# Retention scores: key's rounded part and remainder stacked on 128 partitions

## The reference, cut to what matters

```
def retention(q, k, v, pos):
    q = rope(q, pos)
    k = rope(k, pos) * (dk ** -0.5)
    ...
    def step(state, inp):
        qi, ki, vi = inp
        inner = jnp.einsum('bhid,bhjd->bhij', qi, ki) * decay_mat
        o = jnp.einsum('bhij,bhjv->bhiv', inner, vi) + jnp.einsum('bhid,bhdv->bhiv', qi, state) * q_decay
        ...
```

## Time and profile before

| | us |
|---|---|
| median of 3 runs | 2582.18 (2581.99 to 2584.53) |
| the profiled execution: its own time | 2581.51 |
| the profiled execution: its span | 2579.7 |
| PE busy | 2559.3 (99% of the span) |
| DVE busy | 1103.8 (43%) |
| POOL busy | 1051.2 (41%) |
| ACT busy | 1003.7 (39%) |
| 1976 to 2110 us: PE busy | 133.61 of 134.00, granted clock 1.00 |
| 1976 to 2110 us: ACT, DVE, POOL busy | 73.38, 62.52, 43.41 |

### The profile page before, as it was taken

One profiled execution on the slowest core, in us unless ns is written; L12 is line 12 of the kernel. 1 busy time (PEld: TensorE's weight loads), 2 busy tenths in 40 slices (PEclk: granted clock), 3 DMA queues, 4 the chain that ended last, 5 costly groups with the idle time before them and its releaser, 6 DMA issues.

```text
span 2579.7 us, 35875 instructions
## 1 busy us (share of the span) xinstructions
PE 2559.3 (99%) x12914; PEld 2106.1 (82%) x12914; DVE 1103.8 (43%) x2138; ACT 1003.7 (39%) x1619; POOL 1051.2 (41%) x464
## 2 busy tenths in 40 slices
PE   8999999999999999999999999999999999999998
PEld 7888888887777888888889888889777778888887
DVE  7444336754444135644315544223454455422212
ACT  5222337544454334322334322223555554322321
POOL 0444454342233444544455444453122335344443
PEclk9999999999999999999999999999999999999999
DMA  7455532222222323455532554333112223233232
GB/s 297 157 190 192 179 129 76 66 74 83 90 90 74 106 98 123 168 194 191 179 122 79 199 195 147 99 125 110 50 49 83 86 85 113 68 98 97 94 103 97
DMA packets 78284, 313.15 MB, mean 121 GB/s; under 512 B 9040, under 2 KB 11728, under 8 KB 68720
## 3 DMA queue, kind: packets, MB, share of 16 engines
q1 hardware_dynamic: 65376, 238.09, 27.5%
q10 hardware_dynamic: 12816, 73.80, 8.1%
HBM read 309.72 MB, written 2.13 MB: 121 GB/s over the span
## 4 chain that ended last, share of the span: by engine, by line
PE 96%; DVE 2%; ACT 1%; DMA 0%; POOL 0%; issue 0%; SPq 0%; DVEq 0%; ACTq 0%
PE bank L1955 26%; PE bank L1957 26%; PE bank L1956 26%; PE bank L2007 2%; PE bank L2008 2%; PE bank L2009 2%; PE pair L2223 1%; PE bank L2404 1%; PE pair L2295 1%; PE bank L2282 1%; PE pair L2432 1%; PE bank L2312 1%; PE bank L2412 1%; ACT h_hi L637 0%; PE bank L2488 0%; PE pair L2481 0%
## 5 line engine op out<-in xcount | busy, mean ns | idle before, releaser
L557 POOL TENSOR_TENSOR w_lo<-raw,w_hi 128x1024 fp32r<-128x1024 f32 x412 | 1013.1, 2461 | 1445.6 <-ACT w_hi L596 1445.6
L596 ACT ACTIVATE w_hi<-raw 128x1024 fp32r<-128x1024 f32 x420 | 443.9, 1059 | 1080.9 <-PE bank L1957 1034.2
L1955 PE MATMUL bank<-h_hi,w_hi 128*128 128x512 f32 x2064 | 820.2, 397 | 0.0
L1957 PE MATMUL bank<-h_hi,w_lo 128*128 128x512 f32 x2064 | 804.9, 390 | 0.0
L1956 PE MATMUL bank<-h_lo,w_hi 128*128 128x512 f32 x2064 | 803.8, 389 | 0.0
L1955 PEld LDWEIGHTS bank<-h_hi,w_hi 128*128 128x128 f32 x2064 | 388.0, 188 | 92.7 <-issue 16.3
L1957 PEld LDWEIGHTS bank<-h_hi,w_lo 128*128 128x128 f32 x2064 | 387.5, 188 | 82.7
L1956 PEld LDWEIGHTS bank<-h_lo,w_hi 128*128 128x128 f32 x2064 | 388.1, 188 | 77.2 <-issue 1.2
L1390 DVE TENSOR_TENSOR prod<-bank,rstd 128x512 f32<-128x512 f32 x87 | 60.1, 691 | 428.8 <-PE bank L1957 417.9
L1955 PE MATMUL bank<-act_hi,w_hi 128*128 128x512 f32 x616 | 239.6, 389 | 0.0
L1956 PE MATMUL bank<-act_lo,w_hi 128*128 128x512 f32 x616 | 239.6, 389 | 0.0
(11 more groups left out here) (444 smaller groups left out, 3026.1 us busy)
## 6 DMA issues: line engine op xcount, KB each, us to landing
raw<-slabs_dram SPq DMA_DIRECT2D x420, 512.0 KB, 3.7
adaw<-ada_dram ACTq DMA_DIRECT2D x62, 1024.0 KB, 6.7
ada<-ada_dram SPq DMA_DIRECT2D x8, 1024.0 KB, 20.5
x<-xt_dram SPq DMA_DIRECT2D x4, 512.0 KB, 5.6
adaw<-ada_dram SPq DMA_DIRECT2D x2, 1024.0 KB, 23.6
fneg<-fneg_scratch ACTq DMA_DIRECT2D x4, 512.0 KB, 3.8
sq<-fneg_scratch ACTq DMA_DIRECT2D x4, 512.0 KB, 3.6
w<-w_dram SPq DMA_DIRECT2D x1, 2048.0 KB, 7.9
```

Source lines behind the costliest of these rows:

```text
L557: nc.gpsimd.tensor_tensor(wl[s][:], raw[s][:], wh[s][:], ALU.subtract).then_inc(lo_done, 1)
L596: nc.scalar.activation(wh[s][:], raw[s][:], ACT.Copy).then_inc(hi_done, 1)
L1955: MM(out, wh[s][:, k], a, start=first and j == 0, stop=False)
L1957: ins = MM(out, wl[s][:, k], a, start=False, stop=end and j == len(tiles) - 1)
```

## The change

A buffer `rks[a]` now holds both halves of a head's key on all 128 partitions: the rounded part on the head's own 64 partitions, the remainder on the other 64. The rounded query is written twice (`rqh[a]`, once on each half), the query's remainder once (`rql[a]`), and the other half of `rql[a]` is set to zero once before the first pair. A score is then two matmuls over all 128 rows: `rks` by `rqh` gives hi by hi plus lo by hi, and `rks` by `rql` gives hi by lo. The sum has the same three terms as before. In a group the two matmuls of head 0 come first, then the two of head 1; before, the heads alternated.

`rq_lo_b` lies where `ssacc` is, a buffer that isn't in use during the retention. The first hunk only puts that place on a boundary of 512 bytes.

```
--- before.py
+++ after.py
@@ -224,6 +224,8 @@
             wh.append(sb(f"w_hi{s}", [P, KT, P], F32R))
         for s in range(RING):
             slab_buffers(s)
+        cursor[0] += -cursor[0] % 512
+        ssacc_at = cursor[0]
         ssacc = sb("ssacc", [P, T])
         sq = sb("sq", [P, 2, T])
         rstd = sb("rstd", [P, T])
@@ -312,6 +314,9 @@
 
 
         cursor[0] = shared
+        end, cursor[0] = cursor[0], ssacc_at
+        rql_b = sb("rq_lo_b", [P, T], F32R)
+        cursor[0] = end
         onh = sb("on_hi", [P, NP, T], F32R)
         onl = sb("on_lo", [P, NP, T], F32R)
         orh = sb("or_hi", [P, NP, T], F32R)
@@ -360,8 +365,9 @@
         cursor[0] = m2_at
         rqr = sb("rqr", [P, 2, T])
         rqk = sb("rqk", [P, 2, T])
-        rqkh = sb("rqk_hi", [P, 2, T], F32R)
-        rqkl = sb("rqk_lo", [P, 2, T], F32R)
+        rqh = [sb(f"rq_hi_{z}", [P, T], F32R) for z in "ab"]
+        rql = [sb("rq_lo_a", [P, T], F32R), rql_b]
+        rks = [sb(f"rk_{z}", [P, T], F32R) for z in "ab"]
         rtmp = sb("rtmp", [P, 2, T])
         rcos = sb("rcos", [P, T])
         rsin = sb("rsin", [P, T])
@@ -396,6 +402,9 @@
 
         def halves(h):
             return slice(HALF * h, HALF * (h + 1))
+
+        def head_at(a):
+            return slice(64 * a, 64 * (a + 1))
 
         def scratch(n):
             return (SC0, OV)[n % 2][:, 0:HALF]
@@ -1113,9 +1122,16 @@
 
             def ret_rounded(i):
 
-                for z in range(2):
-                    act.wait_ge(r_qk, 2 * i + z + 1)
-                    nc.scalar.activation(rqkh[:, z], rqk[:, z], ACT.Copy).then_inc(r_qkh, 1)
+                act.wait_ge(r_qk, 2 * i + 1)
+                for a in range(2):
+                    nc.scalar.activation(rqh[a][head_at(a)], rqk[head_at(a), 0], ACT.Copy)
+                for a in range(2):
+                    ins = nc.scalar.activation(rqh[a][head_at(1 - a)], rqk[head_at(a), 0], ACT.Copy)
+                ins.then_inc(r_qkh, 1)
+                act.wait_ge(r_qk, 2 * i + 2)
+                for a in range(2):
+                    ins = nc.scalar.activation(rks[a][head_at(a)], rqk[head_at(a), 1], ACT.Copy)
+                ins.then_inc(r_qkh, 1)
 
             def ret_high(i):
 
@@ -1670,6 +1686,8 @@
                 nsa_pair(c, m, NP - 1, False)
                 c, m = c + 4 * NP, m + 4 * NP
                 dve.wait_ge(r_in, 48)
+                for a in range(2):
+                    V.memset(rql[a].bitcast(F32)[head_at(1 - a)], 0.0)
                 ret_values(0)
                 ret_turned(0, m, 0)
                 ret_turned(1, m, 0)
@@ -1793,9 +1811,14 @@
 
             def ret_low(i):
 
-                for z in range(2):
-                    dve.wait_ge(r_qkh, 2 * i + z + 1)
-                    V.tensor_tensor(rqkl[:, z], rqk[:, z], rqkh[:, z], ALU.subtract).then_inc(r_qkl, 1)
+                dve.wait_ge(r_qkh, 2 * i + 1)
+                for a in range(2):
+                    ins = V.tensor_tensor(rql[a][head_at(a)], rqk[head_at(a), 0], rqh[a][head_at(a)], ALU.subtract)
+                ins.then_inc(r_qkl, 1)
+                dve.wait_ge(r_qkh, 2 * i + 2)
+                for a in range(2):
+                    ins = V.tensor_tensor(rks[a][head_at(1 - a)], rqk[head_at(a), 1], rks[a][head_at(a)], ALU.subtract)
+                ins.then_inc(r_qkl, 1)
 
             def ret_gain(i):
 
@@ -2475,12 +2498,10 @@
                         fill((5, 3, 2, 2)[s - 1])
                         pe.wait_ge(r_ad, 8 * i + 2 * s)
                     if s < TT:
-                        for z, (k, q) in enumerate(((rqkh, rqkh), (rqkh, rqkl), (rqkl, rqkh))):
-                            for a in range(2):
-                                h = slice(64 * a, 64 * (a + 1))
-                                ins = MM(SC[a][:, 0:T - P * s], k[h, 1, P * s:P * (s + 1)], q[h, 0, P * s:T], start=z == 0, stop=z == 2)
-                                if z == 2:
-                                    ins.then_inc(r_s, 1)
+                        for a in range(2):
+                            MM(SC[a][:, 0:T - P * s], rks[a][:, P * s:P * (s + 1)], rqh[a][:, P * s:T], start=True, stop=False)
+                            MM(SC[a][:, 0:T - P * s], rks[a][:, P * s:P * (s + 1)], rql[a][:, P * s:T], start=False, stop=True)\
+                                .then_inc(r_s, 1)
                     if s >= 1:
                         j = s - 1
                         for a in range(2):
```

## The result

The changed kernel takes 2588.84 us, the median of ten runs (2586.8 to 2596.6), against 2582.08 for the kernel before on the same chip (ten runs, 2580.33 to 2584.53). That is 6.8 us more; the ratio is 1.0027, with a 95% interval of 1.002 to 1.0035. The forecast was 2587.0, with a range of its own of 2585.6 to 2589.3. The profiled execution took 2586.91 us (span 2585.0), 5.4 more than that of before.

The account below looks back on a forecast made before the run. PE, with 96% of the chain, was taken to bound the kernel. Operands +5.4 and score groups -0.6 make +4.8 us on 2581.51, 2586.3; the median's 0.67 more gives 2587.0, forecast's own range 2585.6 to 2589.3, overall range 2583.3 to 2590.6.

Parts of the forecast that it names:

- What bounds the kernel, and where the change acts: PE holds 96% of the chain; what counts is score matmul cost and PE's wait for operands before group 0.
- The operands, 5.4 us: ACT's six copies and DVE's four subtractions per pair hold PE up 5.4 us more; bounds +4.5 and +7.2.
- The lag: Per pair, from first rounding copy's start to PE's first score; put at 5.10 us, four pairs 20.4 against 14.97.
- the bounds that the prediction had set (0.63 and 0.69): Upper spacings without overlap for ACT's copies and DVE's subtractions; they give lag 5.55 and +7.2 us.
- the mark of 5.6: Sign for the operands: the prediction is wrong if the lag is below 4.8 or above 5.6 us.
- The score groups, -0.6 us: PE's full-height score matmuls: group 0 zero, group 1 nothing, groups 2 and 3 save 0.14 a pair, 0.6 in four.
- The entry of 0.31: PE's time from the last slab matmul's start to a group's first score in the old kernel, 0.31 us.
- What was cost at nothing: Memsets in DVE's idle time, and later slab rounding, POOL's remainder and gate evacuation: taken as zero.
- cheap half-height work: Rival: 64-partition copies take half of 0.6, or the lag is hidden; lag 4.26, +1.5 us, 2583.5; chance 0.05.
- The drain not saved: Rival: full-height scores pay the old losses, so each group costs a round more; +7.4 us, 2589.6; chance 0.06.
- POOL's case: Rival: POOL's slab remainder starts before DVE's last subtraction and holds it up; lag 7.73, +10.5 us, 2597.5; chance 0.10.
- the faster side: Rival: the new lag stays under 3.5 us and PE sees only its own gain; -1.4 us, 2580.8; chance 0.03.

Follow-up runs that it names:

- the matmuls alone: Kernel before, with its two copies and two subtractions, but four full-height matmuls per score group; 2581.35 us against 2582.78, ratio 0.9994.
- filling the wait: Changed kernel with 14 fills instead of 12 ahead of the operand wait and 3 instead of 5 ahead of group 1; 2583.52 us, ratio 1.0003.
- The three further profiles: The changed kernel as it is, profiled three more times to look at PE's clock; 2591.22, 2592.88 and 2591.88 us.

## Why the prediction came out as it did

**What bounds the kernel, and where the change acts**: right. All of the loss is PE waiting for DVE's last subtraction in front of group 0. Taking away the operands leaves nothing of it (the matmuls alone, -1.4 us), keeping them alone leaves all (+8.8), and filling the wait gives 6.0 of 6.8 us back.

**The operands, 5.4 us**: the step was right and its size too small. The lag was put at 5.10 and is 5.64, so +7.4. The term that failed is the spacing: ACT's copies were taken 0.54 apart where they stay on their partitions, from a 128-partition row, and are 0.645; DVE's subtractions were taken 0.60 apart, from a score evacuation of 128 partitions, and are 0.70. The first error makes 0.2 us of lag (the first subtraction starts 2.59 behind the first copy, put at 2.38), the second 0.3 (the last starts 2.12 behind the first, put at 1.80). Both lay at the bounds that the prediction had set (0.63 and 0.69), the sum of +7.2 there is within 0.2 of what came, and the lag passed the mark of 5.6 at which the prediction called itself wrong by 0.04. The row that was to show that half height overlaps is a copy out of PSUM which begins at partition 0 and is followed by a whole-height one. It showed this for that case alone. For DVE the cause isn't that the row taken reads PSUM. In pair 0 of before, the last step of the rotated key, which reads and writes SBUF on 128 partitions:

```profile
1996.11 0.69 DVE L1792 TENSOR_TENSOR rqk<-rqk,rtmp 128x512 f32<-128x512 f32 x1
```

The query's subtraction, which doesn't need its result, starts 0.61 later. The four new subtractions differ from these in height, and in that each begins on the other half than the one before, as ACT's copies do. No run takes the two apart.

**The score groups, -0.6 us**: right. Groups 1 to 3 save 0.15 a pair (0.14 was worked out): group 1 0.02, group 2 0.06, group 3 0.07. Group 0 behind a wait is 1.00 long instead of 0.90, and the first slab matmul behind it takes 0.23 instead of 0.34, which evens out. Only where no wait is left does group 0 gain too, which the kernel with the matmuls alone shows. The entry of 0.31 ahead of a group is 0.23 now (2034.95 to 2035.18), a slab matmul's own time. With this the trace agrees with the Trainium skill's rule that a change of tiling mode drains the array ("TensorEngine Tiling (Array Packing)", Key Properties): with one change fewer, groups 1 to 3 got 0.02, 0.06 and 0.07 shorter, though each now streams four matmuls in a row where three rounds stood.

**What was cost at nothing**: held. The memsets (0.48 us each) lie in DVE's idle time and PE's only waits are those in front of group 0.

**What was left out: the clock.** The prediction had no term for it. The sum with the measured lags is +6.8 for the retention at full clock, and the profile without a lower stretch there is also the second fastest of the ten runs. The three further profiles are 4.3, 6.0 and 5.0 us slower than that one. Their stretches in the retention make 1.7, 3.4 and 3.4, and each has one more than the first outside it (near 420 us, and twice at 1020), 1.7 again, so that 3.4, 5.1 and 5.1 us are clock.

How much of the median's +6.8 is clock, the mean granted clock of each run tells: 0.9963 over the ten runs of the changed kernel, 0.9964 over the 50 runs of the kernel before in the experiments. The difference is 0.3 us of the span, and the scatter of the ten leaves it uncertain by about 1.3 (one standard error). So the +6.8 is the wait for the most part. The two slowest of the ten, 2594.63 and 2596.6 us, are the two with the lowest clock (0.994 and 0.993). What was wrong in the prediction's sum is the lag, too short by 2.0 us in all. That the median still fell into the forecast's own range is due to the bounds, set at spacings of 0.63 and 0.69, which are close to what came.

**The rivals.** The prediction gave cheap half-height work a time of 2583.5; its own sum, +1.5, makes that 2583.7. The drain not saved (2589.6) lies nearer to the measured time than the forecast and is wrong all the same: the matmuls alone are not slower. POOL's case didn't happen, by 0.31 us. Cheap half-height work and the faster side are refuted by the rows of ACT. Chances of 0.48 for slower and 0.49 for no change were level, and slower it was, by 0.27%.

## What to carry to other kernels

Before an operand is made in more and smaller pieces to save PE a matmul, add up the chain of single instructions that ends in PE's wait, and compare it with the matmuls that stand ahead of that wait. Here half the partitions took as long as all of them (0.63 us on ACT, 0.69 on DVE), and pieces that alternate between the two halves lost the overlap as well: take the spacing from rows of the same engine, height and order of start partitions. A wait on the engine that bounds the kernel can cost more than its length, since a stretch of lower clock may stand behind it; where the order of the work is free, work that is ready goes in front of the wait.

## What the runs showed of the hardware

- ACT's copies of 64x512 from SBUF that begin on partition 0 and 64 in turn go 0.64 to 0.65 us apart, those of 128x512 0.53 to 0.54, each 0.61 to 0.64 long: half the data took a fifth more time. DVE's subtractions do the same, 0.70 against 0.61.
- At waits of 1.7 to 3.8 us PE's granted clock fell to half for about 3.4 us in six of the seven profiles that have waits above 1.8, and not at every such wait: the same kernel showed none, one and two such stretches. In the seven profiles with no wait above 1.8 it did not fall in the retention.
- Full-height matmuls in this format go 0.17 us apart at 384 columns, 0.115 at 256 and 0.11 at 128 (0.07 between the first two): below 256 columns a narrower one is hardly cheaper.
- A subtraction on DVE and a slab's remainder on POOL hold each other up from either side: POOL's took 2.63 instead of 2.40 where DVE's had begun first.
